# Pairs of down-weight slots in one transfer, and hidden units transposed in steps of four

## The chip, the cores and the metric

The kernel runs on one NeuronCore of a Trainium2 chip. The time is the device time of one launch in microseconds (us). The core has TensorE (PE, with its weight loads shown apart as PEld), VectorE (DVE), ScalarE (ACT), GpSimd (POOL), SyncE (SP, which here does nothing but issue transfers), and 16 DMA engines that all queues share.

## What is computed

Two two-layer blocks follow each other; the change touches only the expert part of the second one. In each of its layers, 16 experts pick their tokens (top-k of the affinities) and apply a gated two-layer network; the result is scaled and added back at the tokens' rows. Everything is float32.

```
def ec_moe(h, w_router, w_gate, w_up, w_down):
    ...
    cap = EC_CAPACITY * n_tok // N_EXPERTS
    ...
    xs = jax.vmap(lambda hb, ib: hb[ib])(h, idx)
    hid = jax.nn.silu(jnp.einsum('becd,edf->becf', xs, w_gate)) * jnp.einsum('becd,edf->becf', xs, w_up)
    ye = jnp.einsum('becf,efd->becd', hid, w_down) * g[..., None].astype(h.dtype)
    return jax.vmap(lambda yb, ib: jnp.zeros((n_tok, d), h.dtype).at[ib.reshape(-1)].add(yb.reshape(-1, d)))(ye, idx)
```

Each of `w_gate`, `w_up` and `w_down` is 1024 x 1024 float32 per expert (4.19 MB), so an expert has 12.58 MB of weights. The 512 main tokens give 64 rows to an expert. In layer 0 the 256 context tokens go through the same experts too, with 32 rows each; in layer 1 they don't.

## The kernel before

Engines run their own instruction streams and meet at semaphores. For the experts each engine runs a body for one pair of experts (`u` = 0 and 1) eight times, the first time written out and the rest in a loop.

**Weights.** SP's `body` (L2356 on) issues one transfer per slot: 128 rows of 1024 numbers, 512 KB, 4 KB on each partition. An expert has 24 slots: 0 to 7 gate, 8 to 15 up, 16 to 23 down. Slots 0 to 11 are the `ring`; the other twelve lie in buffers that the attention part has no more use for (`mixT`, `mixcT`, `v`, `probs`, `qz`, `kz`). A slot is loaded again for the next expert as soon as PE has counted (`moe_k`) its last use, so the weights run up to 24 slots ahead of PE. All other weights of the kernel (L307) come in transfers of 512 KB too, but as 1024 runs of 512 bytes (128 x 8 x 128). Only the very first expert of a layer waits for other things (`slot_free`).

**Products.** `product` (L1048) multiplies the stationary activations (64 columns for the main rows, 32 for the context rows) with a slot: two matmuls of 512 columns (L1055), and in layer 0 four more of 256 columns (L1060). The two or four parts of the output stand side by side on different partitions of one PSUM bank, so `hid` is 128 x 512: partitions 0 to 63 hold the hidden columns 0 to 511 of the 64 rows, partitions 64 to 127 the columns 512 to 1023. `hidc` is 128 x 256, in four parts of 32 partitions.

**Between up and down.** PE transposes the next expert's gathered rows (L1042), DVE multiplies the gate's silu with the up product (L1190, and L1193 for the context rows), PE transposes `hid` in four blocks of 128 adjacent columns (L1095) and `hidc` in two (L1100), DVE copies both into `hidT` (L1197, L1202), and PE goes on with the down product. In the trace `hid`, `hidc` and `hidT` all appear as `work`, and the transposed tokens `xsT` as `hT`. PE's wait for `hid` of the main rows, its transposes, its wait for `hidc` and the two transposes stand in this order; the wait for `hidT` is next.

## Time and profile before

| | |
|---|---|
| median of 3 runs | 3107.52 us (3103.11 to 3107.66) |
| profiled execution, first to last instruction | 3105.2 us |
| PE busy | 2721.4 us, 88% of the span |
| DVE / ACT / POOL busy | 33% / 24% / 8% |
| experts of layer 0 | about 1423 to 2070 us |
| experts of layer 1 | about 2558 to 3065 us |

The table is of one execution on the only core. The profile has no other clock than its span, so the span is its own time; it lies 2.3 us under the median of the runs. Busy shares are means over stages with different limits, so the two expert stages are read apart. A DMA share above 1 means that packets of one engine overlap.

### The profile page before, as it was taken

What the parts mean: (1) busy time and instruction counts of PE and PEld (TensorE: products, weight loads), DVE (VectorE), ACT (ScalarE), POOL (GpSimd) and SP (SyncE); (2) the same over time, 40 slices, a digit from 0 to 9 for tenths busy, and PEclk for the clock granted to TensorE, in tenths of its full rate; (3) what the DMA queues carried; (4) which work ended last, traced back from release to release, by engine and by line L of the source; (5) the groups of instructions that cost most, each with busy time, mean ns of one, the idle gap of its engine ahead of it and who ended that gap; (6) DMA issues with size and microseconds to landing.
All of it is one profiled execution on the core that took longest, in us unless ns stands there. A gap on an engine that the chain in (4) does not pass through costs nothing. (4 is left out here: it accounts for less than half of the span.)

```text
span 3105.2 us, 44305 instructions
## 1 busy us (share of the span) xinstructions
PE 2721.4 (88%) x17378; PEld 1465.2 (47%) x17378; DVE 1024.7 (33%) x2278; ACT 745.5 (24%) x1857; POOL 254.5 (8%) x314
## 2 busy tenths in 40 slices
PE   7998999999989899987999999976899969788783
PEld 3664684665867666782222222213666753222221
DVE  3123430224347763553111111126752551011012
ACT  2233411343221453331111111113243321000000
POOL 1000100001000010021000000010000021001001
PEclk9999999999999999987999999997899979999997
DMA  7342614444331011047999999971002059999996
GB/s 217 106 125 67 182 36 114 124 114 120 106 82 34 1 27 48 31 160 278 334 327 330 329 332 331 324 213 39 26 8 75 28 202 387 389 397 396 390 397 233
DMA packets 354638, 579.26 MB, mean 187 GB/s; under 512 B 18592, under 2 KB 242048, under 8 KB 354496
## 3 DMA queue, kind: packets, MB, share of 16 engines
q1 hardware_dynamic: 339040, 523.47, 49.0%
q0 software_dynamic: 15312, 53.67, 6.2%
q8 instruction: 100, 1.64, 0.2%
q14 instruction: 42, 0.34, 0.0%
q10 hardware_dynamic: 144, 0.14, 0.0%
HBM read 554.12 MB, written 23.07 MB: 186 GB/s over the span
## 5 line engine op out<-in xcount | busy, mean ns | idle before, releaser
L441 PE MATMUL ps<-hT,ring 128*128 128x512 f32 x1088 | 482.3, 603 | 5.7 <-ACT hT L1403 4.3
L1055 PE MATMUL ps<-ring,hT 128*64 128x512 f32 x1536 | 424.8, 647 | 63.1 <-DMA ring<-in_w_gate 29.7
L441 PEld LDWEIGHTS ps<-hT,ring 128*128 128x128 f32 x1088 | 209.4, 194 | 264.5 <-issue 257.1
L687 PE MATMUL ps<-ring,mixT 128*128 128x128 f32 x2048 | 232.6, 276 | 0.8 <-DVE mixT L1539 0.8
L1055 PEld LDWEIGHTS ps<-ring,hT 128*64 128x64 f32 x1536 | 86.3, 141 | 308.6 <-DMA ring<-in_w_gate 121.3
L687 PEld LDWEIGHTS ps<-ring,mixT 128*128 128x128 f32 x2048 | 231.0, 193 | 1.3 <-DVE mixT L1539 1.3
L1190 DVE TENSOR_TENSOR work<-work,ps 128x512 f32<-128x512 f32 x32 | 22.0, 688 | 632.3 <-PE ps L1060 326.3
L487 PE MATMUL ps<-kz,qz 96*128 96x256 f32 (+3 forms) x384 | 156.9, 492 | 26.3 <-DVE qz L1965 10.7
L1212 DVE SCALAR_TENSOR_TENSOR hcT<-hcT,gates,work 64x1024 f32<-64x1024 f32 (+1 forms) x48 | 61.3, 1276 | 354.5 <-ACT hcT L1156 221.3
L1126 ACT ACTIVATE hT<-ps,modc 128x64 f32<-128x64 f32 x204 | 62.3, 403 | 400.3 <-PE ps L1042 400.3
L1580 ACT ACTIVATE probsT<-ps 128x512 f32<-128x512 f32 (+3 forms) x280 | 120.3, 455 | 140.2 <-PE ps L527 113.3
L1567 ACT ACTIVATE probs<-ps,col 128x256 f32<-128x256 f32 (+5 forms) x216 | 136.5, 632 | 70.9 <-DVE col L1517 37.0
L513 PE MATMUL ps<-const,probs 128*128 128x128 f32 x752 | 122.9, 280 | 20.5 <-DVE probs L1531 18.4
L1055 PE MATMUL ps<-mixT,hT 128*64 128x512 f32 x512 | 133.4, 612 | 7.0 <-DMA mixT<-in_w_up 6.9
L1513 DVE TENSOR_REDUCE col<-ps 128x1 f32<-128x256 f32 (+4 forms) x136 | 78.9, 580 | 178.1 <-PE ps L487 175.3
L1060 PE MATMUL ps<-ring,hT 128*32 128x256 f32 x1536 | 123.5, 393 | 0.0
L1272 POOL DMA_INDIRECT y_moe<-hcT,idx_to x32 | 46.3, 1447 | 918.2 <-DVE hcT L1212 891.8
L1152 ACT ACTIVATE hcT<-ps 64x512 f32<-64x512 f32 x64 | 37.9, 593 | 338.1 <-PE ps L1060 201.2
L1531 DVE TENSOR_SCALAR probs<-probs,col 128x256 f32<-128x256 f32 (+5 forms) x216 | 112.0, 519 | 7.6
L513 PEld LDWEIGHTS ps<-const,probs 128*128 128x128 f32 x752 | 89.9, 143 | 42.2 <-DVE probs L1531 30.9
L452 PE MATMUL ps<-ring,hT 128*128 128x128 f32 x896 | 103.0, 277 | 4.5 <-ACT hcT L1403 4.5
L452 PEld LDWEIGHTS ps<-ring,hT 128*128 128x128 f32 x896 | 102.8, 194 | 7.7 <-ACT hcT L1403 4.8
(275 smaller groups left out, 3386.3 us busy)
## 6 DMA issues: line engine op xcount, KB each, us to landing
ring<-in_w_gate SPq DMA_DIRECT2D x256, 512.0 KB, 8.9
ring<-in_w_up SPq DMA_DIRECT2D x128, 512.0 KB, 8.7
mixT<-in_w_up SPq DMA_DIRECT2D x128, 512.0 KB, 7.6
ring<-in_w_mod SPq DMA_DIRECT2D x96, 512.0 KB, 5.2
ring<-in_w_in SPq DMA_DIRECT2D x82, 512.0 KB, 7.3
mixcT<-in_w_down SPq DMA_DIRECT2D x64, 512.0 KB, 8.7
qz<-in_w_down SPq DMA_DIRECT2D x64, 512.0 KB, 11.8
kz<-in_w_down SPq DMA_DIRECT2D x64, 512.0 KB, 12.9
```

The costliest lines, as they stand in the source:

```text
L441: mm = nc.tensor.matmul(ps[:, b, 0:n], w[:, k, :], rhs[:, k, 0:n], start=(k == 0), stop=(k == KD - 1))
L452: mm = nc.tensor.matmul(ps[:, b, t * P:(t + 1) * P], lhs[:, k, t * P:(t + 1) * P], w[:, k, :], start=(k == 0), stop=(k == KD - 1))
L487: mm = nc.tensor.matmul(S[:, o:o + rhs.shape[-1]], lhs, rhs, start=lhs is not ident, stop=True, skip_group_check=True)
L513: mm = nc.tensor.transpose(ps[:, 4 + n % 2, i * P:(i + 1) * P], p_sbuf(u)[:, j * P:(j + 1) * P], ident)
L687: mm = nc.tensor.matmul(ps[:, b, c * P:(c + 1) * P], lhs[:, k, tl * P:(tl + 1) * P], ws[c][:, k, :], start=(k == 0), stop=(k == KD - 1))
L1055: mm = nc.tensor.matmul(ps[64 * half:64 * half + 64, dst, :], lhs[:, k, 0:CAP], w[:, half * 512:(half + 1) * 512], start=(k == 0), stop=(k ...
L1060: mm = nc.tensor.matmul(ps[32 * q:32 * q + 32, dstc, 0:256], lhs[:, k, CAP:CAP + CAP_C], w[:, q * 256:(q + 1) * 256], start=(k == 0), stop ...
L1126: ins = nc.scalar.activation(xsT[:, (u + 1) % 2, c, o:o + n], ps[:, 0, c * 96 + o:c * 96 + o + n], ACT.Identity, bias=sh, scale=sc)
L1513: nc.vector.tensor_reduce(nmax(u), s_psum(u), AX, ALU.max, negate=True).then_inc(*done("nmax", u))
L1531: nc.vector.tensor_scalar(p, p, rinv(u), None, ALU.mult).then_inc(*done("probs_normed", u))
L1567: nc.scalar.activation(p_sbuf(u), s_psum(u), ACT.Exp, bias=nmax(u), accum_out=rsum(u)).then_inc(*done("probs", u))
L1580: nc.scalar.activation(probsT[:, n % 2, blocks[0]:blocks[-1] + 1, :], ps[:, 4 + m % 2, 0:len(blocks) * P].rearrange("p (b q) -> p b q", q= ...
```

## The change

The down weights are no longer loaded slot by slot. Their eight slots become four pairs, each of which is one buffer of 2048 numbers a partition (`mixT` first half was slots 12 and 13, and so on: the table `pairs`). One transfer fills a pair. Rows of `w_down` are dealt out in a new way: half of the matrix is 512 rows, partition p gets its rows 4p to 4p+3, and one transfer brings two adjacent ones, 8 KB that lie together in HBM and in the partition. Slot k of the down product now holds rows 4p + (k mod 4) of half k // 4. The row order on the other side must follow: `hid` is transposed in steps of four columns (columns c, c+4, c+8, ...), so that partition p of `hidT` holds hidden column 4p + c. For the context rows a step of four columns in a part of 256 leaves 64 columns, so `hidc` takes four transposes of 64 columns instead of two of 128, and their result, on 64 partitions, goes to `hidT` in two copies of 64 partitions. PE waits for the context rows' `hid` before the first transpose; it waits for a down pair once. The up slots 14 and 15 now use `v` and `probs`.

```diff
--- before.py
+++ after.py
@@ -998,13 +998,16 @@
 
 
         EXPERT_SLOTS = 3 * KD
-        spare = ([mixT[:, 2 * c:2 * c + 2, :].rearrange("p a b -> p (a b)") for c in range(4)]
-                 + [mixcT[:, 4 * c:4 * c + 4, :].rearrange("p a b -> p (a b)") for c in range(2)]
-                 + [v[:, :, :].rearrange("p a b -> p (a b)"), probs[:, D:2 * D]]
-                 + [t[:, 2 * c:2 * c + 2, :].rearrange("p a b -> p (a b)") for t in (qz, kz) for c in range(2)])
+        pairs = [mixT[:, 0:4, :].rearrange("p a b -> p (a b)"), None,
+                 mixT[:, 4:8, :].rearrange("p a b -> p (a b)"), mixcT[:, :, :].rearrange("p a b -> p (a b)"),
+                 qz[:, :, :].rearrange("p a b -> p (a b)"), kz[:, :, :].rearrange("p a b -> p (a b)")]
 
         def expert_slot(s):
-            return ring[:, s, :] if s < RING else spare[s - RING]
+            if s < RING:
+                return ring[:, s, :]
+            if pairs[(s - RING) // 2] is None:
+                return (v[:, :, :].rearrange("p a b -> p (a b)"), probs[:, D:2 * D])[s % 2]
+            return pairs[(s - RING) // 2][:, (s % 2) * D:(s % 2 + 1) * D]
 
         def slot_count(s, l, u, i):
 
@@ -1049,7 +1052,8 @@
 
                 for k in range(KD):
                     s = KD * m + k
-                    pe.wait_ge(sem(f"slot{s}"), slot_count(s, l, u, i))
+                    if m < 2 or k % 2 == 0:
+                        pe.wait_ge(sem(f"slot{s}"), slot_count(s, l, u, i))
                     w = expert_slot(s)
                     for half in range(2):
                         mm = nc.tensor.matmul(ps[64 * half:64 * half + 64, dst, :], lhs[:, k, 0:CAP],
@@ -1090,14 +1094,18 @@
                     pe.wait_ge(sem(f"gathered{(u + 1) % 2}"), count)
                     turn_xs(i, u, u)
 
-                    pe.wait_ge(*at_round("hid", (l, u, 0), i))
+                    if l == 0:
+                        pe.wait_ge(*at_round("hid", (l, u, 1), i))
+                    else:
+                        pe.wait_ge(*at_round("hid", (l, u, 0), i))
                     for c in range(4):
-                        mm = nc.tensor.transpose(ps[:, G, c * P:(c + 1) * P], hid[:, c * P:(c + 1) * P], ident)
+                        mm = nc.tensor.transpose(ps[:, G, c * P:(c + 1) * P],
+                                                 hid.rearrange("p (x j) -> p j x", j=4)[:, c, :], ident)
                     mm.then_inc(*done("hid_turned", (l, u, 0)))
                     if l == 0:
-                        pe.wait_ge(*at_round("hid", (l, u, 1), i))
-                        for c in range(2):
-                            mm = nc.tensor.transpose(ps[:, GC, c * P:(c + 1) * P], hidc[:, c * P:(c + 1) * P], ident)
+                        for c in range(4):
+                            mm = nc.tensor.transpose(ps[0:64, GC, c * P:(c + 1) * P],
+                                                     hidc.rearrange("p (x j) -> p j x", j=4)[:, c, :], ident)
                         mm.then_inc(*done("hid_turned", (l, u, 1)))
                     pe.wait_ge(*at_round("hidT", (l, u), i))
 
@@ -1197,9 +1205,10 @@
                     ins = nc.vector.tensor_copy(dst, src)
                     if l == 0:
                         dve.wait_ge(*at_round("hid_turned", (l, u, 1), i))
-                        dst = hidT.rearrange("p (a j) t -> p j a t", a=4)[:, :, :, CAP:CAP + CAP_C]
-                        src = ps[:, GC, 0:256].rearrange("p (j a t) -> p j a t", j=2, a=4)
-                        ins = nc.vector.tensor_copy(dst, src)
+                        for q in range(2):
+                            dst = hidT[64 * q:64 * q + 64].rearrange("p (a j) t -> p j a t", a=2)[:, :, :, CAP:CAP + CAP_C]
+                            src = ps[0:64, GC, :].rearrange("p (j a q t) -> p j a q t", j=4, a=2, q=2)[:, :, :, q, :]
+                            ins = nc.vector.tensor_copy(dst, src)
                     ins.then_inc(*done("hidT", (l, u)))
                     dve.wait_ge(*at_round("xs_turned", (l, u, 1), i))
                     modulate(i, u, u)
@@ -2357,11 +2366,22 @@
                         for m, w in enumerate((a["w_gate_2"], a["w_up_2"], a["w_down_2"])):
                             for k in range(KD):
                                 s = KD * m + k
+                                if m == 2 and k % 2:
+                                    continue
+                                used = s + (m == 2)
                                 if first_round(i) and u == 0:
                                     slot_free(s)
                                 else:
 
-                                    sp_.wait_ge(sem("moe_k"), i * 48 + (base + EXPERT_SLOTS * (u - 1) + s + 1))
+                                    sp_.wait_ge(sem("moe_k"), i * 48 + (base + EXPERT_SLOTS * (u - 1) + used + 1))
+                                if m == 2:
+                                    half = slice((k // 4) * 512, (k // 4 + 1) * 512)
+                                    src = w[l, e, half, :] if first_round(i) else (
+                                        w[l, bass.ds(e, 1), half, :].rearrange("o r n -> (o r) n"))
+                                    src = src.rearrange("(p j) n -> p j n", j=4)[:, k % 4:k % 4 + 2, :]
+                                    sp_.dma_start(pairs[(s - RING) // 2].rearrange("p (j n) -> p j n", j=2),
+                                                  src).then_inc(sem(f"slot{s}"), 16)
+                                    continue
                                 if first_round(i):
                                     src = w[l, e, k * P:(k + 1) * P, :]
                                 else:
```

On PE, layer 0, at the seam between an expert's up and down product (`mixT,hT` is the end of the up product, then the next expert's tokens, the two sorts of transposes, and the down product), before:

```order
893 L1042 MATMUL ps<-const,hT 128x96 x8
894 L1095 MATMUL ps<-const,work 128x128 x4
895 L1100 MATMUL ps<-const,work 128x128 x2
896 L1055 MATMUL ps<-mixcT,work 64x512 x2
897 L1060 MATMUL ps<-mixcT,work 32x256 x4
```

and now:

```order
893 L1045 MATMUL ps<-const,hT 128x96 x8
894 L1102 MATMUL ps<-const,work 128x128 x4
895 L1107 MATMUL ps<-const,work 64x128 x4
896 L1059 MATMUL ps<-mixT,work 64x512 x2
897 L1064 MATMUL ps<-mixT,work 32x256 x4
```

The context rows' transposes are four with an output of 64 partitions instead of two with 128; the order is the same.

On DVE, layer 0, at the same seam (multiply, multiply, copies into `hidT`, then the next expert's tokens), before:

```order
1138 L1190 TENSOR_TENSOR work<-work,ps 128x512
1139 L1193 TENSOR_TENSOR work<-work,ps 128x256
1140 L1197 COPY work<-ps 128x4x2x64
1141 L1202 COPY work<-ps 128x2x4x32
1142 L1174 TENSOR_SCALAR hT<-ps,modc 128x64
```

and now:

```order
1138 L1198 TENSOR_TENSOR work<-work,ps 128x512
1139 L1201 TENSOR_TENSOR work<-work,ps 128x256
1140 L1205 COPY work<-ps 128x4x2x64
1141 L1211 COPY work<-ps 64x4x2x32 x2
1142 L1182 TENSOR_SCALAR hT<-ps,modc 128x64
```

One copy of 128 partitions has become two of 64 partitions, each with as many numbers on a partition as the one before had.

On SP, the up and down transfers of one expert, before:

```order
33 L2369 DMA ring<-in_w_up 128x1024 x4
34 L2369 DMA mixT<-in_w_up 128x1024 x4
35 L2369 DMA mixcT<-in_w_down 128x1024 x2
36 L2369 DMA v<-in_w_down 128x1024
37 L2369 DMA probs<-in_w_down 128x1024
38 L2369 DMA qz<-in_w_down 128x1024 x2
39 L2369 DMA kz<-in_w_down 128x1024 x2
```

and now:

```order
33 L2389 DMA ring<-in_w_up 128x1024 x4
34 L2389 DMA mixT<-in_w_up 128x1024 x2
35 L2389 DMA v<-in_w_up 128x1024
36 L2389 DMA probs<-in_w_up 128x1024
37 L2382 DMA mixT<-in_w_down 128x2048
38 L2382 DMA mixcT<-in_w_down 128x2048
39 L2382 DMA qz<-in_w_down 128x2048
40 L2382 DMA kz<-in_w_down 128x2048
```

Eight down transfers of 128 x 1024 have become four of 128 x 2048, whose 2048 numbers are one run on each side.

## Rows read from the trace of the kernel before

**Rows 1.** The page's GB/s in 40 slices of the span.

```profile
GB/s 217 106 125 67 182 36 114 124 114 120 106 82 34 1 27 48 31 160 278 334 327 330 329 332 331 324 213 39 26 8 75 28 202 387 389 397 396 390 397 233
```

**Rows 2.** Busy time of two stretches: layer 0's experts, layer 1's.

```profile
core 0: us, PE busy (x) PEld busy (x) DVE busy (x) ACT busy (x) POOL busy (x), PEclk, DMA share, GB/s
1500.00:2000.00 500.00, 488.12 (x3722) 121.05 (x3720) 80.30 (x170) 73.79 (x198) 33.44 (x48) 1.00 0.95 329
2700.00:3000.00 300.00, 240.68 (x978) 60.85 (x976) 33.48 (x64) 28.02 (x64) 24.73 (x36) 0.96 1.03 394
```

**Rows 3.** What SP's queue waited for, 1500 to 2000 us: total, times, longest.

```profile
SPq L2369 <- PE ps L1060: 345.7, 296, 3.8
```

**Rows 4.** PE in order of time, at one seam of layer 0 and the next.

```profile
1735.22 0.88 PE L1042 MATMUL ps<-const,hT 96*128 96x96 f32 x8
1736.19 0.65 PE L1095 MATMUL ps<-const,work 128*128 128x128 f32 x4
1736.68 0.38 PE L1100 MATMUL ps<-const,work 128*128 128x128 f32 x2
1737.96 1.08 PE L1055 MATMUL ps<-mixcT,work 128*64 128x512 f32 x4 [0.90 <-DVE work L1202]
...
1778.59 0.65 PE L1055 MATMUL ps<-mixcT,work 128*64 128x512 f32 x2 [0.90 <-DVE work L1202]
```

**Rows 5.** DVE in order of time at the first of these seams.

```profile
1735.45 0.69 DVE L1190 TENSOR_TENSOR work<-work,ps 128x512 f32<-128x512 f32 x1 [19.82 <-PE ps L1060]
1736.05 0.41 DVE L1193 TENSOR_TENSOR work<-work,ps 128x256 f32<-128x256 f32 x1
1736.88 0.69 DVE L1197 COPY work<-ps 128x512 f32<-128x512 f32 x1 [0.42 <-PE ps L1095]
1737.49 0.41 DVE L1202 COPY work<-ps 128x256 f32<-128x256 f32 x1
1737.82 1.97 DVE L1174 TENSOR_SCALAR hT<-ps,modc 128x64 f32<-128x64 f32 x8
```

**Rows 6.** Who waited for whom, 2650 to 3000 us: total, times, longest.

```profile
PEld ps L1055 <- DMA ring<-in_w_gate: 95.3, 82, 1.9
```

**Rows 7.** Transfers, 2700 to 3000 us: GB/s in 40 slices; an issue, last its us to landing.

```profile
GB/s 406 344 409 409 410 347 411 409 408 387 367 409 410 409 343 409 410 410 376 376 409 407 410 348 410 410 411 358 385 411 410 409 341 410 410 408 348 410 410 410
...
mixcT<-in_w_down SPq DMA_DIRECT2D x18, 512.0 KB, 17.9
```

**Rows 8.** Transfers, 160 to 176 us, 512-byte runs: GB/s in 40 slices.

```profile
GB/s 0 0 0 0 0 0 0 0 0 0 0 0 0 0 0 0 0 41 0 0 0 15 96 155 303 344 348 343 307 289 283 289 293 296 291 289 291 287 292 274
```

**Rows 9.** The page's queues: one whose packets are 16 KB.

```profile
q8 instruction: 100, 1.64, 0.2%
```

**Rows 10.** SP in order of time where layer 1's experts begin.

```profile
2530.74 0.96 SPq L2369 DMA_DIRECT2D kz<-in_w_down  x2
2559.75 2.04 SPq L2369 DMA_DIRECT2D ring<-in_w_gate  x2
```

**Rows 11.** PE in order of time: two seams, layer 1.

```profile
2821.57 0.71 PE L1042 MATMUL ps<-const,hT 64*128 64x64 f32 x8
...
2824.14 1.94 PE L1055 MATMUL ps<-mixcT,work 128*64 128x512 f32 x8 [0.97 <-DVE work L1197]
2825.88 1.06 PE L1055 MATMUL ps<-v,work 128*64 128x512 f32 x4
...
2854.86 0.71 PE L1042 MATMUL ps<-const,hT 64*128 64x64 f32 x8
```

**Rows 12.** Weight loads by shape: busy us, mean ns, idle.

```profile
L441 PEld LDWEIGHTS ps<-hT,ring 128*128 128x128 f32 x1088 | 209.4, 194 | 264.5 <-issue 257.1 <-ACT hT L1403 5.1 <-ACT hT L1390 2.1
...
L702 PEld LDWEIGHTS ps<-diag,const 128*128 128x128 f32 x96 | 18.2, 251 | 11.2 <-DVE diag L1639 5.1 <-POOL diag L1639 3.4 <-issue 2.1
...
L1095 PEld LDWEIGHTS ps<-const,work 128*128 128x128 f32 x128 | 13.4, 141 | 10.2 <-DVE work L1190 10.2
```

**Rows 13.** PE in order of time: the last slot of the last expert.

```profile
3063.40 0.20 PEld L1055 LDWEIGHTS ps<-kz,work 128*64 128x64 f32 x4 [1.02 <-DMA kz<-in_w_down]
```

## The prediction

> **What bounds the kernel now.** I read the page's slices first: only the stretches at 324 to 334 GB/s (layer 0's experts) and at 387 to 397 (layer 1's) move enough data for a change of weight transfers to matter [rows 1]. Then I split busy time by these two stretches [rows 2].
>
> Layer 0 is bound by TensorE: 488.1 of 500 us busy, full granted clock. SP's queue spends 345.7 of the 500 us waiting for PE to free a slot [rows 3]. The weights arrive at 329 GB/s because PE takes them at that rate; the other stage shows that the engines can do more. So nothing that makes transfers cheaper is felt here. One expert takes 40.63 us (the down product begins at 1737.96 and, one expert later, at 1778.59), and PE's only gap in it is 0.90 us, ended by DVE's second copy, L1202 [rows 4]. What lengthens the chain from the up product through DVE, the transposes and the copies to the down product lengthens the layer one for one, 16 times.
>
> Layer 1 is bound by the transfers. Its matmuls wait for gate weights for 95.3 us in 350, up to 1.9 us at a time [rows 6], the DMA share is 1.03 [rows 2], and the rate stands flat at 409 to 411 GB/s, with dips to about 345 where an expert's gather and scatter run between [rows 7]. Two seams lie 33.3 us apart [rows 11]. PE's stops at the seam are hidden here: PE waits for data again right after. The first expert's 24 slots were all issued by 2531 us, before its products begin; the stream starts again at 2559.75 [rows 10], so 15 experts are paced by the transfers.
>
> **The change, part by part.** The sum is made against the profiled 3105.2 us, 2.3 us under the median of the runs, 3107.5.
>
> *Layer 0, the later start of the transposes.* Now L1095 starts at 1736.19 [rows 4], 0.05 us after L1190 ends at 1736.14 [rows 5]. In the changed kernel PE waits for L1193 as well, which ends at 1736.05 + 0.41 = 1736.46. The transposes start at 1736.51, 0.32 us later. Only L1100's successor stood behind that wait before; now the four main transposes do too, and behind them DVE's copies.
>
> *Layer 0, two transposes more.* Four transposes take 0.49 us from start to start of the next group (1736.19 to 1736.68), and DVE's copy starts 0.69 us after the first. So the first copy starts at 1737.20. The four context transposes start at 1737.00 and, priced like the 0.65 us of the other four, end by 1737.65. DVE can take the second copy only 0.61 us after the first (1736.88 to 1737.49 [rows 5]), at 1737.81. The extra transposes are covered by 0.16 us; without that cover they would cost 0.65 - 0.38 = 0.27 us.
>
> *Layer 0, one copy more.* Each half copy has 256 numbers a partition, as the single L1202 has, so I take its 0.41 us although only 64 partitions work. The next DVE instruction follows it after 0.33 us (1737.49 to 1737.82 [rows 5]). The second half runs from 1738.14 to 1738.55, and PE goes on 0.06 us later, as now (1737.90 to 1737.96). The down product starts at 1738.61 instead of 1737.96: **+0.65 us an expert, +10.4 us for 16.**
>
> *The step of four columns.* `hid` is the weight side of the transposes, and its 128 columns are now read 16 bytes apart. No row shows such a load. The adjacent one takes 141 ns [rows 12]. The bounds: 0 extra, or 53 ns as in the 194 ns of an ordinary load of the same shape, which puts 4 x 53 = 0.21 us an expert on the chain (3.4 us in layer 0); the slowest load of this shape, 251 ns, is the far end. I take half of the 53 ns, since nothing in the rows chooses between the two: **+1.8 us**. Layer 1 hides it. The Trainium skill ("SBUF — State Buffer", Specifications) says that SBUF is organised in lines of 16 bytes that want two hits each for full bandwidth. By that rule a step of 16 bytes takes the full penalty, with no price given; by the adjacent row it takes none. The two sums differ by the 3.4 us.
>
> *Layer 1, the transfers.* An expert brings 12.58 MB. At the flat 410 GB/s each of 16 engines takes 16 x 4096 / 410e9 = 159.8 ns for a run of 4 KB. Where the kernel loads runs of 512 bytes without pause the rate is about 290 GB/s [rows 8], 28.2 ns a run. The line through both is 9.4 ns a run plus 36.7 ns a KB. A run of 8 KB then costs 310.2 ns against 319.6 for two. That it can be one packet is supported by packets of 16 KB on another queue (1.64 MB in 100) [rows 9], and by the order, where source and destination are each one run of 2048. Down weights are 8 slots x 8 runs on an engine, 32 pairs: 32 x 9.4 ns = 0.30 us, and four completion writes fewer, about 0.04 us. **-0.34 us an expert, -5.1 us for 15.** The bounds: nothing, if the packets stay at 4 KB; at the other end the down third free of dips and at the highest rate of a slice, 411: that recovers a third of the difference between the flat 410 and the mean 394 [rows 2], 0.43 us, and with the 0.34 it makes 0.77 us, -11.6 us.
>
> *Waits and slots.* PE waits for a pair instead of a slot, and SP issues a pair only when its second slot is free. A slot passes in 0.87 us on PE in layer 1 (two slots from 2824.14 to 2825.88 [rows 11]) and the stream runs 24 slots ahead with some 14 in flight (17.9 us to landing [rows 7] by 1.28 us each). Hidden, in both layers. What a thinner cover would cost is one slot, 0.87 us. At the very end nothing hides it: the last slot's product now starts at 3063.40, when it lands [rows 13]. As a pair, slot 22 must be multiplied after that too: **+0.9 us, once.**
>
> Removed waits (four of eight per down product) and 4 fewer issues an expert on SP cost or give nothing: PE issues ahead, SP waits anyway. The first round's checks guard the same buffers.
>
> Sum: 10.4 + 1.8 - 5.1 + 0.9 = **+8.0 us**, 3107.5 + 8.0 = 3115.5 us.
>
> **The rivals.**
>
> *Not slower: the pairs pay more than the line says.* Reads of 8 KB could also shorten the dips and stalls. For no change within 0.2% the gain must be 6.9 us (13.1 less 6.2), 0.46 us an expert; to be faster by 0.2% it needs 19.3 us, 1.29 us an expert, more than a tenth of the 10.2 us of the down third. With the bound above, 11.6 us, the time is 3107.5 + 13.1 - 11.6 = 3109.0. For it: the dips are a real loss of 1.3 us an expert. Against: they belong to gather and scatter, whose bytes stay. Chance 0.24, of which 0.09 faster. The layer 0 chain being shorter than I add up (a copy of 64 partitions taking less) acts the same way.
>
> Beside this stands a rule of the Trainium skill ("DMA: Bandwidth & Descriptors", Anatomy of one DMA): about 2 us fixed for a transfer plus its bytes at 436 GB/s, and the advice to make transfers of 1 MiB or more. By it four pairs instead of eight slots would save an estimated 8 us an expert, 120 us in all. The trace speaks against it: single slots of 512 KB already pass at 410 GB/s, 1.28 us each, since many are in flight.
>
> *Packets stay at 4 KB, no gain.* 3107.5 + 13.1 = 3120.6. Chance 0.08.
>
> *The new addresses are read more slowly.* One transfer now takes 8 KB out of every 16 KB. If the down third ran at the lowest slice, 341 GB/s [rows 7], 4.19 MB would take 12.3 us instead of 10.2: +2.1 us, 31 us for 15 experts, and no gain: 3152. Against: the loads of 512-byte pieces with far larger gaps run at 290 GB/s, on the line of the run's size. Chance 0.05.
>
> *The step costs as the slowest load.* 110 ns on each load: 0.44 us for the main four, and the context four end late by up to 0.3 us: 3107.5 + 16 x 1.39 + 0.9 - 5.1 = 3125.5. Chance 0.03.
>
> **How the numbers follow.** A measurement tells about 0.2%, 6.2 us, from no change. The forecast has 0.60; its own range is 3110 to 3119 (the step 0 to 3.4 us, the gain 3 to 8 us, the half copies 0.05 us less or more each), of which about a quarter lies within 0.2%: 0.45 slower, 0.15 same. Slower: 0.45 + 0.08 + 0.05 + 0.03 = 0.61; same: 0.15 + 0.15 = 0.30; faster 0.09. The range, 3106 to 3122, leaves out the pitch, the slowest load and the faster end of the first rival.
>
> **What would show it.** In layer 0: the seam's gap; the wait of the down product is for the second half copy; an expert takes 41.3 to 41.5 us. Right if the main transposes start 0.3 us after their place now. In layer 1: packets of 8 KB, slices without a dip at or just above 410 to 415 GB/s, two seams 32.9 to 33.0 us apart. The prediction is wrong if layer 1's period falls by more than 0.5 us, if it grows, or if layer 0's grows by less than 0.4 or more than 1.1 us.

## The result and the profile after

The change made the kernel slower: 3122.15 us (median of 4 runs, 3116.85 to 3123.32) against 3107.01, a ratio of 1.0047 with an interval of 1.0033 to 1.0061. That is 15.1 us, where 8.0 were forecast. The profiled execution spans 3120.3 us.

The page of the changed kernel, with its 40 slices, answers to [rows 1]:

```profile
span 3120.3 us, 44075 instructions
...
PE 2724.9 (87%) x17410; PEld 1472.4 (47%) x17410; DVE 1030.7 (33%) x2294; ACT 745.4 (24%) x1857; POOL 254.2 (8%) x314
...
GB/s 215 106 125 62 185 35 115 126 111 122 103 81 34 1 33 41 39 175 267 326 320 323 320 329 317 307 222 69 19 15 75 21 190 377 394 401 401 393 402 227
```

PE has nearly the same work as before (2724.9 us against 2721.4) in a span 15 us longer. The slices of layer 0's experts now read 317 to 329 GB/s where they read 324 to 334, those of layer 1's up to 402 where the top was 397. The two stages apart, as in [rows 2]: busy time, granted clock, DMA share and GB/s.

```profile
1500.00:2000.00 500.00, 481.68 (x3648) 122.02 (x3646) 83.94 (x181) 71.11 (x192) 33.36 (x48) 0.99 0.92 321
2700.00:3000.00 300.00, 239.23 (x988) 62.77 (x984) 32.99 (x63) 27.68 (x63) 24.67 (x36) 0.97 1.03 398
```

In 500 us of layer 0 PE is busy for 6.4 us less, its mean granted clock is 0.99 instead of 1.00, and the rate fell from 329 to 321 GB/s; in layer 1 it rose from 394 to 398. Both signs were forecast.

PE in order of time at a seam of layer 0, to be set beside [rows 4]; the last number in brackets is the idle time and what ended it:

```profile
1743.49 0.88 PE L1045 MATMUL ps<-const,hT 96*128 96x96 f32 x8
1744.79 0.75 PE L1102 MATMUL ps<-const,work 128*128 128x128 f32 x4 [0.42 <-DVE work L1201]
1745.38 0.60 PE L1107 MATMUL ps<-const,work 128*64 128x128 f32 x4
1747.08 1.08 PE L1059 MATMUL ps<-mixT,work 128*64 128x512 f32 x4 [1.10 <-DVE work L1211]
```

The tokens' transposes start at 1743.49; the down product 3.59 us later, where it took 2.74 before (1735.22 to 1737.96). DVE at the same seam, beside [rows 5]:

```profile
1743.72 0.69 DVE L1198 TENSOR_TENSOR work<-work,ps 128x512 f32<-128x512 f32 x1 [19.82 <-PE ps L1064]
1744.32 0.41 DVE L1201 TENSOR_TENSOR work<-work,ps 128x256 f32<-128x256 f32 x1
1745.58 0.69 DVE L1205 COPY work<-ps 128x512 f32<-128x512 f32 x1 [0.84 <-PE ps L1102]
1746.19 0.84 DVE L1211 COPY work<-ps 64x256 f32<-64x256 f32 x2
1747.06 1.98 DVE L1182 TENSOR_SCALAR hT<-ps,modc 128x64 f32<-128x64 f32 x8
```

From the start of DVE's multiply to the start of the main transposes it is now 1.07 us (0.74 before): the wait for L1201. From there to the first copy it is 0.79 (0.69 before). From the first copy to the down product it is 1.50 (1.08 before), for the two half copies. 0.33 + 0.10 + 0.42 = 0.85 us. The weight loads of the transposes by shape, beside [rows 12] (the second line is for the context rows):

```profile
L1102 PEld LDWEIGHTS ps<-const,work 128*128 128x128 f32 x128 | 17.9, 210 | 15.6 <-DVE work L1201 9.6 <-DVE work L1198 5.9
...
L1107 PEld LDWEIGHTS ps<-const,work 128*64 128x64 f32 x64 | 7.6, 141 | 0.0
```

A load of the same 128 columns went from 141 to 210 ns.

The spacing of the experts shows these 0.85 us again, and more. From the second start of token transposes (1453.31) to the seventeenth (2078.45) there are 625.14 us, 41.68 an expert against 40.62; with 0.85 more it would be 41.47. Thirteen of the fifteen spacings are 41.38 to 41.48, and two, the tenth and the fourteenth, are 43.06 and 43.05. One of these two, PE in order of time:

```profile
1828.33 0.60 PE L1107 MATMUL ps<-const,work 128*64 128x128 f32 x4
1830.03 1.72 PE L1059 MATMUL ps<-mixT,work 128*64 128x512 f32 x4 [1.10 <-DVE work L1211]
1831.69 1.08 PE L1064 MATMUL ps<-mixT,work 128*32 128x256 f32 x8
1832.70 1.58 PE L1059 MATMUL ps<-mixT,work 128*64 128x512 f32 x4
1834.21 0.64 PE L1064 MATMUL ps<-mixT,work 128*32 128x256 f32 x8
```

The same matmuls that take 1.08 us for four and 0.64 for eight elsewhere take 1.72 and 1.08 here, until about 1834. The granted clock of the stretch says why (the number ahead of the last two; the second line is from the seam at 1747.08, which has no fall):

```profile
1829.00:1833.00 4.00, 2.97 (x14) 0.70 (x16) 2.94 (x11) 0.40 (x2) 0.00 (x0) 0.67 0.55 217
1747.00:1751.00 4.00, 3.92 (x28) 0.91 (x28) 2.00 (x9) 0.00 (x0) 0.00 (x0) 1.00 0.37 147
```

It fell from full (2.4 GHz) to half (1.2 GHz) just after the seam's last idle time; the mean of the 4 us is 0.67. What that costs is the 1.58 us between 43.06 and 41.48. At no seam of the profiled execution before is there such a fall.

In layer 1, the rates and packets answer to [rows 7]:

```profile
GB/s 420 415 410 346 414 422 409 383 368 423 411 410 345 417 418 409 369 389 422 412 405 352 419 416 410 340 416 421 407 375 382 423 412 410 340 417 419 409 354 400
DMA packets 27772, 119.55 MB, mean 398 GB/s; under 512 B 3216, under 2 KB 3216, under 8 KB 23145
...
mixcT<-in_w_down SPq DMA_DIRECT2D x9, 1024.0 KB, 19.3
```

4627 packets are of 8 KB: 27772 less the 23145 smaller ones. Slices without a dip now reach up to 423 GB/s, where 411 was the top before. Thirteen experts from 2640.48 to 3069.06 are 32.97 us apart, against 33.27 before (2621.78 to 3054.25).

### The profile page after: what moved, and what is told of

The parts are those of the page before. It is cut to its first block and busy times, and to the rows that moved or that the text cites. A ratio compares the mean times of both kernels' runs of the same rounds, so it can differ in the third digit from the quotient of the medians.

```text
span 3120.3 us, 44075 instructions
## 1 busy us (share of the span) xinstructions
PE 2724.9 (87%) x17410; PEld 1472.4 (47%) x17410; DVE 1030.7 (33%) x2294; ACT 745.4 (24%) x1857; POOL 254.2 (8%) x314
## 5 line engine op out<-in xcount | busy, mean ns | idle before, releaser
L1059 PE MATMUL ps<-ring,hT 128*64 128x512 f32 x1536 | 416.6, 635 | 58.9 <-DMA ring<-in_w_up 40.5
L1576 ACT ACTIVATE probs<-ps,col 128x256 f32<-128x256 f32 (+5 forms) x216 | 136.5, 632 | 70.2 <-DVE col L1526 36.7
L1064 PEld LDWEIGHTS ps<-ring,hT 128*32 128x32 f32 x1536 | 30.3, 108 | 157.4 <-issue 157.4
## 6 DMA issues: line engine op xcount, KB each, us to landing
mixcT<-in_w_down SPq DMA_DIRECT2D x32, 1024.0 KB, 10.6
```

Source lines behind the costliest of these rows:

```text
L1059: mm = nc.tensor.matmul(ps[64 * half:64 * half + 64, dst, :], lhs[:, k, 0:CAP], w[:, half * 512:(half + 1) * 512], start=(k == 0), stop=(k ...
L1064: mm = nc.tensor.matmul(ps[32 * q:32 * q + 32, dstc, 0:256], lhs[:, k, CAP:CAP + CAP_C], w[:, q * 256:(q + 1) * 256], start=(k == 0), stop ...
L1576: nc.scalar.activation(p_sbuf(u), s_psum(u), ACT.Exp, bias=nmax(u), accum_out=rsum(u)).then_inc(*done("probs", u))
```

## The experiments

Times are medians of rounds in which the kernel before ran in turn with the others. There were four sessions, each on a chip of its own, and the kernel before had 3107.33, 3106.26, 3107.16 and 3107.14 us in them: the first with pairs alone, transposes alone, gap filled and quarters; the second with early wait, adjacent columns, one half copy and pairs for all; the third with the three kernels marked "again"; the fourth with short runs. Between sessions the ratios are to be compared, not the times. "Clock falls" counts, in the profiled execution, the seams of layer 0 with a fall of the granted clock behind them. "Spacing" is the time between the tokens' transposes of consecutive experts on PE, in layer 0 over 15 experts, in layer 1 over the last 13. These two tell far more than the medians, since single executions of one kernel differ by 10 us and more, and the first token transposes of layer 0 alone, before any expert's seam, start between 1416.6 and 1424.8 us in the fourteen profiles.

| kernel | us | ratio, 95% interval | layer 0 spacing | clock falls | layer 1 spacing |
|---|---|---|---|---|---|
| before | | 1 | 40.62 | 0 | 33.27 |
| changed | 3122.2 | 1.0047 (1.0033 to 1.0061) | 41.68 | 2 | 32.97 |
| changed again | 3122.6 | 1.0051 (1.0038 to 1.0064) | 41.78 | 3 | 33.04 |
| pairs alone | 3104.3 | 0.9988 (0.9979 to 0.9998) | 40.62 | 0 | 33.04 |
| transposes alone | 3121.1 | 1.0044 (1.0030 to 1.0059) | 41.78 | 3 | 33.23 |
| early wait | 3113.1 | 1.0021 (1.0011 to 1.0031) | 41.13 | 0 | 33.00 |
| adjacent columns | 3113.4 | 1.0021 (1.0012 to 1.0030) | 41.37 | 0 | 32.94 |
| adjacent columns again | 3117.0 | 1.0034 (1.0021 to 1.0047) | 41.37 | 0 | 32.99 |
| one half copy | 3112.3 | 1.0015 (1.0005 to 1.0025) | 41.03 | 0 | 32.92 |
| gap filled | 3118.2 | 1.0036 (1.0024 to 1.0047) | 41.46 | 0 | 32.92 |
| quarters | 3106.2 | 0.9993 (0.9983 to 1.0003) | 40.70 | 0 | 32.92 |
| quarters again | 3105.3 | 0.9996 (0.9986 to 1.0005) | 40.70 | 0 | 32.91 |
| pairs for all | 3102.7 | 0.9991 (0.9981 to 1.0001) | 40.70 | 0 | 32.60 |
| pairs, short runs | 3107.1 | 1.0001 (0.9990 to 1.0011) | 40.62 | 0 | 33.29 |

**Pairs alone.** From the changed kernel, transposes, wait and copies are put back:

```diff
-                    if l == 0:
-                        pe.wait_ge(*at_round("hid", (l, u, 1), i))
-                    else:
-                        pe.wait_ge(*at_round("hid", (l, u, 0), i))
+                    pe.wait_ge(*at_round("hid", (l, u, 0), i))
...
-                        for c in range(4):
...
+                        pe.wait_ge(*at_round("hid", (l, u, 1), i))
+                        for c in range(2):
...
-                        for q in range(2):
```

> The pairs of down slots and their one wait a pair, with the transposes, copies and waits of the kernel before. The hidden units then meet other rows of the down weights than they should, so the output is another one; the work is the same. Theory A (the seam of layer 0 costs 0.85 us an expert plus falls of the clock, the pairs gain 0.29 us on each of 15 experts and lose 0.9 us at the end): 3107.0 - 4.3 + 0.9 = 3103.6 us, layer 0's experts 40.62 us apart, layer 1's 32.9. Rival B (a part of the 15 us comes from the transfers of 1 MB themselves, for instance through PE in layer 0): 3107 us or more, and experts of layer 0 more than 40.7 us apart.

3104.3 us: 3.1 less than the kernel before, with layer 0's spacing the same to 0.01 us. The transfers of 1 MB cost layer 0 nothing. Rival B is out: all of the loss is in the rest of the change.

**Transposes alone.** The kernel before with the later wait, the transposes in steps of four and the half copies:

```diff
+                    if l == 0:
+                        pe.wait_ge(*at_round("hid", (l, u, 1), i))
...
+                                                 hid.rearrange("p (x j) -> p j x", j=4)[:, c, :], ident)
...
+                        for q in range(2):
```

> The new transposes, the later wait and the two half copies, with the loads of the kernel before slot by slot (output not the reference's, rows of the down weights are not rearranged). Theory A: 16 x 0.85 = 13.6 us, and one to three falls of the clock at 1.6 us: 3121 to 3126 us; layer 0's experts 41.47 us apart, layer 1's 33.2. Rival B: clearly under 3117 us.

3121.1 us, 13.7 more than before. Without the falls the spacing is 41.46 to 41.48; three experts had one. With the pairs alone the two halves add to -3.1 + 13.7 = 10.6 us where the changed kernel has 15.1 and 15.4. These 4 to 5 us are within the doubt of the medians: by the intervals, pairs alone is 0.6 to 6.5 us faster and transposes alone 9.3 to 18.3 us slower. The profiles leave no such gap. From the first token transposes of layer 0 to the end of the span it is 1685.7 us before, 1683.4 with pairs alone and 1702.6 with transposes alone; -2.3 and +16.9 add to 14.6, and the changed kernel's two profiles have +12.7 (two falls) and +15.4 (three).

**Early wait.** PE waits for the context rows' units before the fourth transpose:

```diff
-                    if l == 0:
-                        pe.wait_ge(*at_round("hid", (l, u, 1), i))
-                    else:
-                        pe.wait_ge(*at_round("hid", (l, u, 0), i))
+                    pe.wait_ge(*at_round("hid", (l, u, 0), i))
                     for c in range(4):
+                        if l == 0 and c == 3:
+                            pe.wait_ge(*at_round("hid", (l, u, 1), i))
```

> The changed kernel, but PE waits for the main rows' hidden units before the first transpose and for the context rows' before the fourth, so that the later wait is undone. Theory A (seam = 0.33 us wait + 0.10 us loads + 0.42 us copies): experts of layer 0 41.14 us apart instead of 41.47, 5.3 us less than the changed kernel, about 3117 us. Rival D (the wait is hidden by the rest of the chain): 41.4 us apart and 3121 to 3122 us.

PE in order of time at one seam:

```profile
1743.27 0.88 PE L1045 MATMUL ps<-const,hT 96*128 96x96 f32 x8
1744.23 0.75 PE L1101 MATMUL ps<-const,work 128*128 128x128 f32 x4
1744.82 0.60 PE L1106 MATMUL ps<-const,work 128*64 128x128 f32 x4
1746.52 1.08 PE L1059 MATMUL ps<-mixT,work 128*64 128x512 f32 x4 [1.10 <-DVE work L1210]
```

The spacing is as expected, 41.13, so the wait is worth 0.33 us an expert. The 1.10 us of idle time ahead of the down product are still there, but the 0.42 us before the main transposes are gone, and this profile has no fall. The kernel is 6.8 us slower than the kernel before, where the changed one is 15.1: a difference of 8.3 us, not 5.3.

**Adjacent columns, twice.** Only the step is undone:

```diff
-                                                 hid.rearrange("p (x j) -> p j x", j=4)[:, c, :], ident)
+                                                 hid[:, c * P:(c + 1) * P], ident)
...
-                                                     hidc.rearrange("p (x j) -> p j x", j=4)[:, c, :], ident)
+                                                     hidc[:, c * 64:(c + 1) * 64], ident)
```

> The changed kernel with both sorts of transposes reading adjacent columns (128 and 64 at a time), so that only the step of four is undone; the hidden units then meet other rows, so the output is another one. Theory A: weight loads 140 ns instead of 211, the copy starts 0.10 us earlier, experts of layer 0 41.37 us apart, 1.6 us less: about 3120.5 us. Rival E (the step costs more than the loads show, for instance in the matmuls): 41.2 us apart or less, under 3119 us.

> The changed kernel itself, on the same chip and in the same rounds as the next two, because the kernels without the late wait and without the step of four came out 8 to 9 us under it instead of 5.3 and 1.6. Theory A with the clock: experts of layer 0 41.47 us apart, two or three of them 43.05, 3120 to 3123 us; the rest of the difference to the other two kernels is falls of the clock that they don't have. Rival H (chips and sessions differ by that much): 3115 to 3118 us with the same seams.

> The changed kernel with adjacent columns in the transposes (output another one, as before), a second look. Theory A: 41.37 us apart, no falls again, and in these rounds 1.6 us less than the changed kernel for the loads plus 1.6 us for each fall that the changed kernel has (5 to 7 us in all). Rival I (falls strike any of these kernels at random): falls appear here too, and the two medians lie 1 to 2 us apart.

Weight loads of this kernel, by shape:

```profile
L1102 PEld LDWEIGHTS ps<-const,work 128*128 128x128 f32 x128 | 13.4, 140 | 15.5 <-DVE work L1201 9.6 <-DVE work L1198 5.9
...
L1107 PEld LDWEIGHTS ps<-const,work 128*64 128x64 f32 x64 | 7.0, 111 | 0.0
```

140 ns, and the spacing is 41.37 us: the step costs 0.10 us an expert, as theory A has it. In neither profile is there a fall, in both profiles of the changed kernel there are (two and three). Rival I is out, too: three profiles with the step of four have 8 falls in 48 seams, these two have none in 32. In the same rounds the medians are 5.6 us apart (3122.6 and 3117.0); 1.6 us for the loads and three falls of 1.58 us would make 6.3. The first 3113.4 us were a miss (3120.5 expected): I had not reckoned with the falls going away. The two medians of this kernel are 3.5 us apart with the same seams in both profiles. The profiled executions differ by 4.4 us, and 3.7 of them lie before the first token transposes of layer 0 (1420.62 and 1424.29), so this is not the seam's. The changed kernel repeated its 3122; rival H is out.

**One half copy.**

```diff
-                        for q in range(2):
+                        for q in range(1):
```

> The changed kernel without the second of the two half copies: half of the context rows' hidden units keep the values of an earlier expert, so the output is another one. Theory A: the down product starts 0.42 us earlier, experts 41.05 us apart, 6.7 us less, and fewer or no falls of the clock: 3112 to 3115 us. Rival F (DVE's next work fills the time and delays PE anyhow): 41.3 us or more apart.

41.03 us and 3112.3 us: 0.43 us an expert for a half copy, 6.9 us with its 16, and no fall in the profile. PE's last idle time at the seam is 0.67 us here.

**Gap filled.**

```diff
                         mm.then_inc(*done("hid_turned", (l, u, 1)))
+                        for c in range(6):
+                            nc.tensor.transpose(ps[:, U, 0:P], ident, ident)
```

> The changed kernel with six transposes of the identity, into a bank that is free at that time, between the context rows' transposes and the wait for the copies, in layer 0. PE's idle time there should shrink from 1.1 to about 0.4 us while the down product starts at the same time. Theory A with the clock: no falls of the granted clock at the seams of layer 0, experts 41.5 us apart throughout, about 3107.0 + 13.6 - 3.4 = 3117.2 us. Rival C (the falls have nothing to do with the idle time at the seam): as many falls as in the changed kernel, and its time, 3120 to 3123 us.

PE in order of time at a seam of this kernel:

```profile
1747.40 0.60 PE L1107 MATMUL ps<-const,work 128*64 128x128 f32 x4
1747.83 0.82 PE L1111 MATMUL ps<-const 128*128 128x128 f32 x6
1749.10 1.08 PE L1059 MATMUL ps<-mixT,work 128*64 128x512 f32 x4 [0.45 <-DVE work L1213]
```

The idle time ahead of the down product is 0.45 us instead of 1.10, the start of the product is as late as before (3.59 us after 1745.51), and there is no fall. The median is 3118.2 us against 3122, which is what two or three falls cost, but the intervals of the two ratios overlap. That the falls come from the idle time at the seam is supported, not proven, and rival C has this profile against it: the seams lie in time as in the changed kernel. At one seam in six, as in the changed kernel and transposes alone, 16 seams without a fall would come by chance about once in twenty.

**Quarters, twice.** A pair is 256 adjacent rows, two adjacent ones on each partition. `hid` and `hidc` are then transposed in steps of two, with instructions as many and as large as before the change:

```diff
-                                    half = slice((k // 4) * 512, (k // 4 + 1) * 512)
+                                    half = slice((k // 2) * 256, (k // 2 + 1) * 256)
...
-                                    src = src.rearrange("(p j) n -> p j n", j=4)[:, k % 4:k % 4 + 2, :]
+                                    src = src.rearrange("(p j) n -> p j n", j=2)
...
+                                                 hid.rearrange("p (m x j) -> p m j x", m=2, j=2)[:, c // 2, c % 2, :], ident)
...
+                        pe.wait_ge(*at_round("hid", (l, u, 1), i))
+                        for c in range(2):
...
+                                                     hidc.rearrange("p (x j) -> p j x", j=2)[:, c, :], ident)
```

> Another deal of the rows: a pair is a quarter of the down weights, 256 rows, of which partition p gets rows 2p and 2p+1. The transfer is 1 MB without holes in HBM, the transposes go in steps of two columns (8 bytes), the context rows need two transposes of 128 columns and one copy as before, and PE's first wait is for the main rows' hidden units alone, as before. The output is the reference's. Theory A: the seam as before (40.6 us an expert), the gain of the pairs kept: about 3103.6 us. If a step of two slows the weight loads as the step of four does (211 ns instead of 141), the seam grows by up to 0.1 us: 3105. Rival B: 3107 or more.

> The quarters version a second time, to narrow its interval against the kernel before. Theory A: experts of layer 0 40.71 us apart (0.09 us more than before, 1.4 us in all), of layer 1 32.9 (0.3 us less, 4.7 us in all), 0.6 back at the end: 2.7 us less than the kernel before, ratio 0.9991. Rival: no difference.

Its loads, by shape:

```profile
L1099 PEld LDWEIGHTS ps<-const,work 128*128 128x128 f32 x128 | 17.7, 207 | 10.2 <-DVE work L1196 10.2
...
L1105 PEld LDWEIGHTS ps<-const,work 128*128 128x128 f32 x32 | 5.3, 209 | 0.0
```

A step of two numbers costs a load nearly as much as a step of four, 207 ns against 210. The spacing in layer 0 is 40.70 us, 0.09 more than before, in layer 1 32.92, 0.35 less. The medians are 1.1 and 1.9 us under the kernel before, both intervals hold 1. So it keeps what the pairs give and loses little at the seam, and it is 17 us faster than the changed kernel in the same rounds; that it beats the kernel before is what the spacings say and the medians don't prove.

**Pairs for all.** From the quarters version, gate and up weights go in pairs as well:

```diff
+                                single = s in (14, 15)
+                                if k % 2 and not single:
+                                    continue
...
+                                dst = (ring[:, s:s + 2, :] if s < RING
+                                       else pairs[(s - RING) // 2].rearrange("p (j n) -> p j n", j=2))
```

> The quarters version with 11 pairs: gate and up slots are loaded two a transfer as well, in the same deal of the rows, but for up slots 14 and 15, whose buffers are not adjacent. The tokens are left in their order, so the gate and up products meet other rows and the output is another one; PE, DVE and ACT do the same work as in the quarters version. Theory A (a gain for each run of 8 KB): 0.29 us x 11/4 = 0.8 us an expert of layer 1, 32.4 us apart, 12 us less than 3107.3 and 0.9 back at the end: about 3097 us. Rival G (the gain of the down pairs has another source, such as one wait less on PE or the order of buffers): about 3105 us, 32.9 us apart.

Its rates and packets in layer 1:

```profile
GB/s 417 334 415 425 419 360 407 421 422 385 371 423 423 425 348 417 422 421 368 385 423 421 386 383 426 423 419 331 416 424 419 376 388 421 423 387 376 425 421 421
DMA packets 18686, 120.87 MB, mean 403 GB/s; under 512 B 2205, under 2 KB 2205, under 8 KB 5661
```

Slices without a dip now reach 421 to 426 GB/s, and the spacing is 32.60, 0.67 us under the kernel before where 0.8 to 0.9 was expected; the pairs' gain is 0.06 us each here and 0.08 to 0.09 in the quarters version. Transfers land 25 to 29 us after their issue, where it was 15 to 18. At the quarters version's 0.0875 us a pair, 11 pairs would give 0.96 us; why nearly a third of that is missing wasn't settled. The median is 3102.7, not 3097: that was a miss too, and its interval still holds 1.

**Pairs, short runs.** From pairs alone, the source is two blocks of 128 rows:

```diff
-                                    half = slice((k // 4) * 512, (k // 4 + 1) * 512)
+                                    half = slice(k * P, (k + 2) * P)
...
-                                    src = src.rearrange("(p j) n -> p j n", j=4)[:, k % 4:k % 4 + 2, :]
+                                    src = src.rearrange("(j p) n -> p j n", j=2)
```

> Down slots in pairs of one transfer of 1 MB, but each partition gets one row from each of two blocks of 128 rows, so that the runs stay at 4 KB (128 x 2 x 1024); transposes, copies and waits as in the kernel before; the output is the reference's. It holds the number and size of transfers, the one wait a pair and the late last pair of the changed kernel and leaves out the runs of 8 KB. Theory A (the gain is per run): no gain, layer 1's experts 33.2 us apart, slices flat at 410 GB/s, 0.6 to 0.9 us more than before at the end. Rival J (the gain comes from fewer, larger transfers): 32.9 to 33.0 us apart, about 3104 us.

```profile
GB/s 410 338 410 410 410 379 375 411 409 410 332 410 410 410 376 376 411 410 410 342 410 409 410 354 400 410 409 401 350 409 410 410 352 407 411 409 380 375 410 411
DMA packets 32072, 118.36 MB, mean 395 GB/s; under 512 B 3178, under 2 KB 3178, under 8 KB 32072
```

No slice passes 411 GB/s, all packets are of 4 KB or less, the spacing is 33.29 and the time 3107.1, that of the kernel before. Half as many down transfers of twice the size give nothing. This kernel differs from pairs alone in the order of the source rows only, so the gain is that of the 8 KB runs.

## Why the prediction was right in sign and too low in size

The forecast of 8.0 us is 7.1 short. By the two profiles of the changed kernel, the seam makes 1.4 us of it in both, the clock 3.2 and 4.7, what layer 1 gained less than forecast 1.2 and 2.6, and code that is the same 1.3 more and 1.3 less.

**The signs that the prediction set itself came out**: the main transposes start 0.33 us later, the down product waits for the second half copy, the spacing without falls is 41.47 us in layer 0 and 32.97 in layer 1, and the packets are of 8 KB.

**The bounds of the stages were right.** What lengthened the seam lengthened layer 0 one for one; what shortened transfers shortened layer 1 alone. Pairs alone left layer 0 at 40.62 us; transposes alone left layer 1 at 33.23.

**The later wait** was priced at 0.32 us and measured 0.33.

**The transposes** were taken as hidden, and they are: the context four end at 1745.98, 0.2 us before the half copy can start.

**The half copies** were mis-sized. One copy more was priced at 0.33 us by its distance to the next instruction in [rows 5]; the whole change of that step is 0.42. The 0.33 held for instructions that overlap by 0.08 us: L1202 ended at 1737.90, and the next one had started at 1737.82. The first half copy still overlaps L1205 so (it starts at 1746.19, L1205 ends at 1746.27). The second one doesn't overlap the first (0.84 us for two of 412 ns), nor does the instruction behind it. Both halves have 64 partitions, so the width is not the reason; what differs is that the second writes from partition 64 on. No run tests that.

**The step of four** was bounded by 0 and 53 ns a load with half of it taken, 1.8 us in all (half of 3.4 is 1.7, a slip). It is 70 ns a load. Of four times that, 0.28 us, only 0.10 us an expert comes through, 1.6 us in all. Right in the sum by luck, since two errors cancel: the load was above my upper bound, and about a third of it reached the chain where I let through all.

**The sum of the seam** is then 0.85 us where 0.76 was forecast (10.4 + 1.8 over 16): 13.6 us against 12.2.

**The step that is missing is the clock.** "What lengthens the chain ... lengthens the layer one for one, 16 times" holds at a constant clock. PE's idle time at the seam grew from 0.90 us, alone, to 0.42 and 1.10 us, and in two or three experts of an execution the granted clock fell behind it, 1.58 us each: 3.2 us in the profiled execution, 4.7 in the second one. The sum had nothing for it.

**The pairs** were priced at -0.34 us an expert. The changed kernel has -0.30 (33.27 to 32.97) and once -0.23. The forecast took it 15 times. The runs show it in the last 13 spacings; the first three take 67.0 and 67.2 us where they took 66.4. So all of layer 1, from its first token transposes to the end of the span, takes 546.9 and 548.2 us against 549.8: 3.0 and 1.6 us less, where -5.1 + 0.9 = -4.2 was forecast. The line through 512 bytes and 4 KB gave 310 ns for a run of 8 KB (its 36.7 ns a KB are for 1000 bytes), which at 16 engines is 423 GB/s; slices show 421 to 426. Its counterpart is the rule of the Trainium skill ("DMA: Bandwidth & Descriptors", Anatomy of one DMA) that each transfer has about 2 us of its own; the page fits it to transfers issued from GpSimd, and these are issued by SP. It does not govern here: with as few and as large transfers but short runs, the gain is nil.

**The end** was priced at +0.9. From the last token transposes to the end it is 51.2 us against 51.0, so +0.2; in the other profiles of kernels with pairs it is 0.6 to 0.9 more. PE in order of time over the last down product:

```profile
3071.54 1.94 PE L1059 MATMUL ps<-mixT,work 128*64 128x512 f32 x8 [0.78 <-DVE work L1205]
...
3075.03 1.89 PE L1059 MATMUL ps<-qz,work 128*64 128x512 f32 x8
3077.34 1.94 PE L1059 MATMUL ps<-kz,work 128*64 128x512 f32 x8 [0.43 <-DMA kz<-in_w_down]
```

The last pair lands 0.43 us after PE is through with the one before, and both of its slots follow.

Added up for the profiled execution: 13.6 + 3.2 for layer 0, less 0.3 x 13 = 3.9 for the last 13 spacings of layer 1, and 0.2 at the end make 13.1 us; 2.4 more were there before the first expert (its tokens' transposes start at 1421.92 against 1419.51), in code that is the same and in which executions differ anyhow; the rest, -0.4, is between the layers and at the start of layer 1. The second profile has three falls and no such late start (1419.47), and is 15.4 us longer than the profile before. Of the rivals, that of gains beyond the line, the 4 KB packets, the slow addresses and the slow loads are all refuted by the packets and the spacings. The result, 3122.15 us, lies at the very edge of the range, 3122, which reached there for the sake of those rivals and not for the clock: that it comes so near is luck.

## What to carry to other kernels

In a stage where one engine has no slack, read what an edit adds between two of its matmul bursts instruction by instruction, and then ask of the clock as well: idle time that grows from 0.9 to 1.5 us came with falls that cost more than its own length in three profiles, though not in two others. With some 14 transfers in flight, as here, the price of a transfer lay in the length of its contiguous runs and not in its size; deal the rows so that the runs get longer without a new shape for the consumer. Here 256 adjacent rows a transfer did that, and 512 did not. Two edits that pull opposite stages are best timed apart: the medians of 3104 and 3121 us showed what the 3122 hid.

## What the runs showed of the hardware that was not expected

- A weight load of 128 float32 columns takes 141 ns from adjacent columns, 207 with a step of two (8 bytes) and 210 with a step of four (16 bytes). The Trainium skill ("SBUF — State Buffer", Specifications) has lines of 16 bytes that want two hits each for full bandwidth; by it the step of two, with two hits a line, should be as fast as adjacent columns. The measurement decides: here it is not. For 64 columns it is 111 ns adjacent against 141 with a step of four.
- The granted clock fell from 2.4 to 1.2 GHz for about 3 us after two separated idle times of 0.42 and 1.10 us, in 2 to 3 seams of 16 (three profiles); none was seen after one of 0.90 us, after 1.10 us without the 0.42, nor with 0.42 and 0.45 or 0.42 and 0.67. With adjacent columns the idle times are the same 0.42 and 1.10 us, and in two profiles no fall is to be seen. So the idle time doesn't decide alone whether and where a fall comes; what does was not settled. It is not mere chance: the changed kernel's second profile and transposes alone have their falls in the same three of fifteen spacings, the fourth, the seventh and the eleventh.
- Two VectorE copies of 64 x 256 numbers in a row take 0.84 us, 412 ns each, when the first writes to partitions 0 to 63 and the second to 64 to 127, with no overlap; a copy of 128 x 256 behind one of 128 x 512 starts 0.08 us before that one ends.
- A run of 8 KB passes as one packet, at 421 to 426 GB/s over 16 engines in slices without a dip when 22 of 24 slots are loaded so; runs of 4 KB at 409 to 411.
